# Scan of an RWKV recurrence: half of the heads change partition halves from level to level, and the inverse's factor is identity plus power

## What is computed

```python
def rwkv_step(S, inp):
    r, w, k, v, kk, a = inp
    sa = jnp.einsum('dbhvk,dbhk->dbhv', S, -kk)
    S = S * w[..., None, :] + sa[..., :, None] * (kk * a)[..., None, :] + v[..., :, None] * k[..., None, :]
    y = jnp.einsum('dbhvk,dbhk->dbhv', S, r)
    return S, y
```

## Time and profile before

| what | value |
|---|---|
| time, median of 3 runs | 4139.14 us (4133.52 to 4139.69) |
| time of the profiled execution | 4142.12 us |
| its span | 4140.3 us |
| granted clock, mean over the span | 0.936 |
| TensorE busy | 3631.0 us, 88% |
| VectorE busy | 2830.5 us, 68% |
| ScalarE busy | 1609.6 us, 39% |
| stage of the scan in the span | about 2785 to 3175 us |

### The profile page before, as it was taken

The page is one execution under the profiler, slowest core; times in us unless marked ns, Lnnn a source line. Parts: engine busy times, 40 slices in busy tenths (PEclk is TensorE's granted clock), DMA queues, the critical chain, the costliest instruction groups (busy, mean ns, idle before and its releaser), DMA issues. The chain is left out here.

```text
span 4140.3 us, 62371 instructions
## 1 busy us (share of the span) xinstructions
PE 3631.0 (88%) x24735; PEld 2927.8 (71%) x24735; DVE 2830.5 (68%) x3464; ACT 1609.6 (39%) x2136; POOL 72.4 (2%) x56
## 2 busy tenths in 40 slices
PE   6999996879959999948999776649999897999897
PEld 4888885767848888836888432319997676888786
DVE  4775325977559999978886588685555557667356
ACT  3222212545537777754333120253333133322244
POOL 0000000000020000010000000000000000000000
PEclk8999998999969999978999888779999998999999
DMA  5942225536579999953332331340111332222565
GB/s 199 337 166 92 88 76 194 192 112 214 181 278 420 413 411 411 399 194 102 102 122 102 124 123 69 117 166 26 42 34 63 102 117 77 82 91 73 187 192 170
DMA packets 262498, 689.49 MB, mean 167 GB/s; under 512 B 30136, under 2 KB 126072, under 8 KB 235754
## 3 DMA queue, kind: packets, MB, share of 16 engines
q1 hardware_dynamic: 226474, 559.75, 37.8%
q10 hardware_dynamic: 20528, 67.11, 4.3%
q0 software_dynamic: 15248, 59.14, 3.9%
HBM read 530.81 MB, written 172.96 MB: 170 GB/s over the span
## 5 line engine op out<-in xcount | busy, mean ns | idle before, releaser
L157 PE MATMUL g_ps<-h1T_hi,g_w_lo 128*128 128x512 f32 x448 | 175.4, 392 | 6.9 <-DVE g_w_lo L356 6.9
L1775 DVE TENSOR_TENSOR moe_wg_lo<-moe_wg,moe_wg_hi 128x2048 fp32r<-128x2048 f32 x68 | 153.1, 2288 | 35.6 <-ACT moe_wg_hi L1629 35.5
L159 PE MATMUL g_ps<-h1T_hi,g_w_hi 128*128 128x512 f32 x448 | 174.8, 390 | 0.0
L158 PE MATMUL g_ps<-h1T_lo,g_w_hi 128*128 128x512 f32 x448 | 174.8, 390 | 0.0
L4164 DVE TENSOR_TENSOR x3T_lo<-fd_w_raw,x3T_hi 128x1024 fp32r<-128x1024 f32 x66 | 80.8, 1224 | 122.6 <-ACT x3T_hi L4093 122.4
L1775 DVE TENSOR_TENSOR moe_wu_lo<-moe_wu,moe_wu_hi 128x2048 fp32r<-128x2048 f32 x68 | 152.9, 2288 | 16.3 <-ACT moe_wu_hi L1629 16.3
L1775 DVE TENSOR_TENSOR moe_wd_lo<-moe_wd,moe_wd_hi 128x2048 fp32r<-128x2048 f32 x66 | 148.3, 2289 | 14.9 <-ACT moe_wd_hi L1629 14.9
L2882 PE MATMUL rs_banks<-rs_pm,rs_qx 64*64 64x64 f32 x2048 | 157.2, 217 | 0.0
L157 PE MATMUL fd_acc<-x3T_hi,x3T_lo 128*128 128x512 f32 x352 | 139.2, 395 | 19.9 <-DVE x3T_lo L4167 19.9
L157 PE MATMUL g_ps<-x2T_hi,g_w_lo 128*128 128x512 f32 x352 | 139.8, 397 | 17.1 <-DVE g_w_lo L583 17.1
L157 PE MATMUL g_ps<-g_w_hi,h1T_lo 128*128 128x512 f32 x384 | 149.6, 390 | 0.0
(11 more groups left out here) (738 smaller groups left out, 10776.4 us busy)
## 6 DMA issues: line engine op xcount, KB each, us to landing
moe_wg<-in_exp_w_gate SPq DMA_DIRECT2D x68, 1024.0 KB
moe_wu<-in_exp_w_up SPq DMA_DIRECT2D x68, 1024.0 KB
moe_wd<-in_exp_w_down SPq DMA_DIRECT2D x66, 1024.0 KB
fd_w_raw<-in_ffn_w_down SPq DMA_DIRECT2D x66, 512.0 KB, 4.5
go_w_raw<-in_w_out SPq DMA_DIRECT2D x64, 512.0 KB, 4.4
g_w<-in_w_in SPq DMA_DIRECT2D x52, 512.0 KB, 4.8
g_w<-in_w_in SPq DMA_DIRECT2D x22, 1024.0 KB, 7.7
s_xs<-g_zero POOLq DMA_DIRECT2D x2, 8192.0 KB, 34.3
```

The costliest lines, as they stand in the source:

```text
L157: pe.matmul(out, l[1], r[0], start=(k == 0), stop=False)
L158: pe.matmul(out, l[0], r[1], start=False, stop=False)
L159: return pe.matmul(out, l[0], r[0], start=False, stop=(k == kt - 1))
L1775: v.tensor_tensor(lo[:, q * m:q * m + m], w[:, q * m:q * m + m], hi[:, q * m:q * m + m], ALU.subtract).then_inc(sem_lo, 1)
```

## The change

- Placement: a matrix of parity 0 stays in `home[b]`; one of parity 1 lies in `home[b]` at even levels and in the other half at odd ones (`place`). A product of parity 1 thus reads one half and writes the other, and the four kinds of matrices of a group use the four quadrants of the array.
- Groups are by direction (d = g) instead of parity.
- `qx` and `pm` become one tile `px` with three columns of 64: `pm`, `qm`, `xm`. PSUM has the three side by side too, one bank for each group and parity (`powers_of`).
- X is raised by `(I + power) X` in one product: `rx` = power + identity is made by VectorE at each level from 0 to 4, and the product of the next level has `rx` as weights. VectorE no longer adds the product to X; the new X comes with the copies.
- Each matrix has three matmuls of 64 columns at levels 1 to 3 instead of one of 128 and one of 64.
- Copies: for group 0 ScalarE copies parity 0 and VectorE parity 1, for group 1 ScalarE copies both; each copy has two or three times 64 columns for two slots (level 5: one times 64). VectorE's two adds for `rx` follow its copy and wait for ScalarE's copies.
- The first X is written in four operations instead of two, the parity-1 half of them into the other half of the partitions.

```diff
-        sc, pm, qx = s.sb("sc", [P, 2, ND, 2, P]), s.sb("pm", [P, ND, RC]), s.sb("qx", [P, ND, P])
+        sc, px = s.sb("sc", [P, 2, ND, 2, P]), s.sb("px", [P, ND, 3 * RC])
+        pm, qm, xm = (px[:, :, c * RC:c * RC + RC] for c in range(3))
+        rx, eye = s.sb("rx", [P, ND, RC]), s.sb("eye", [P, RC])
...
+        def powers_of(g, par):
+
+            return banks[:, 2 * g + par].rearrange("p n c -> p (n c)")[:, 0:6 * RC].rearrange("p (n c) -> p n c", c=3 * RC)
...
+        def columns(lv):
+
+            return slice(0, 2 * RC) if lv == 0 else slice(0, 3 * RC) if lv < NL - 1 else slice(2 * RC, 3 * RC)
+
+        def own(ap, g, par):
+
+            return ap[:, par * RP + 2 * g:par * RP + 2 * g + 2]
...
+        def place(b, par, lv):
+
+            return other[b] if par and lv % 2 else home[b]
...
                 if n:
-                    for g in range(2):
-                        pe.wait_ge(lv_dve, past(dve_level(n - 1, NL - 1, g)))
+                    pe.wait_ge(lv_act, past(act_at(n - 1, NL - 1, 3)))
+                    pe.wait_ge(lv_dve, past(dve_at(n - 1, NL - 1)))
...
                 for g in range(2):
                     if lv == 0:
                         pe.wait_ge(sc_ok, past(2 * n + 2))
+                        pe.wait_ge(p0_ok, past(n + 1))
                     else:
-                        if lv < NL - 1:
-                            pe.wait_ge(lv_q, past(q_level(n, lv - 1, g)))
-                        pe.wait_ge(lv_p1 if g else lv_p0, past(p_level(n, lv - 1)))
+                        pe.wait_ge(lv_act, past(act_at(n, lv - 1, 3 if g else 1)))
+                        if g == 0:
+                            pe.wait_ge(lv_dve, past(dve_at(n, lv - 1)))
+                    members = [(par * RP + g * 2 + a, a, b, par) for a in range(2) for par in range(2) for b in range(2)]
+
+                    def power(k, a, b, par):
+                        o = place(b, par, lv)
+                        return sc[o, n % 2, g * RP + 2 * a + b, par, 0:RC] if lv == 0 else qm[o, k]
+
+                    def to(a, b, par, c):
+                        return powers_of(g, par)[place(b, par, lv + 1), a, c * RC:c * RC + RC]
+                    if lv < NL - 1:
+                        for k, a, b, par in members:
+                            mm = pe.matmul(to(a, b, par, 0), power(k, a, b, par), pm[place(b, par, lv), k], start=True, stop=True)
+                    if lv < NL - 2:
+                        for k, a, b, par in members:
+                            mm = pe.matmul(to(a, b, par, 1), pm[place(b, par, lv), k], power(k, a, b, par), start=True, stop=True)
+                    if lv:
                         if lv == 1:
-                            pe.wait_ge(x1_ok, past(2 * n + 2))
-                        else:
-                            pe.wait_ge(lv_dve, past(dve_level(n, lv - 1, g)))
-                    for e in range(RP):
-                        for b in range(2):
-                            d, p, o, k = e // 2, e % 2 * 2 + b, home[b], g * RP + e
-                            q = sc[o, n % 2, d * RP + p, g, 0:RC] if lv == 0 else qx[o, k, 0:RC]
-                            if lv == 0:
-                                pe.matmul(p_q[g][o, e, 0:RC], pm[o, k], q, start=True, stop=True)
-                            elif lv < NL - 2:
-                                pe.matmul(p_q[g][o, e], pm[o, k], qx[o, k], start=True, stop=True)
-                            else:
-                                mm = pe.matmul(p_q[g][o, e, RC:P], pm[o, k], qx[o, k, RC:P], start=True, stop=True)
-                            if lv < NL - 1:
-                                mm = pe.matmul(p_p[g][o, e], q, pm[o, k], start=True, stop=True)
+                            pe.wait_ge(x1_ok, past(4 * n + 4))
+                        pe.wait_ge(lv_r, past(r_at(n, lv - 1, g)))
+                        for k, a, b, par in members:
+                            o = place(b, par, lv)
+                            mm = pe.matmul(to(a, b, par, 2), rx[o, k], xm[o, k], start=True, stop=True)
                     mm.then_inc(level, 1)
...
             def raise_power(n, lv):
-                for g in range(2):
-                    k = slice(g * RP, g * RP + RP)
+                c = columns(lv)
+                for g, par in ((0, 0), (1, 0), (1, 1)):
                     act.wait_ge(level, past(at_level(n, lv, g)))
-                    if lv < NL - 2:
-                        act.activation(qx[:, k, 0:RC], p_q[g][:, :, 0:RC], ACT.Copy).then_inc(lv_q, 1)
-                act.activation(pm[:, k], p_p[1][:, 0:RP], ACT.Copy).then_inc(lv_p1, 1)
+                    act.activation(own(px[:, :, c], g, par), powers_of(g, par)[:, :, c], ACT.Copy).then_inc(lv_act, 1)
...
+            for o in half:
+                v.tensor_copy(eye[o], ident[o, o])
+            v.drain()
...
                 for b in range(2):
-                    o = home[b]
-                    v.tensor_tensor(by_parity(qx[o])[:, :, :, RC:P], sides(sc[o, n % 2, :, :, 0:RC], b),
-                                    bc(ident[o, o].unsqueeze(1).unsqueeze(1), [64, 2, RP, RC]), ALU.add).then_inc(x1_ok, 1)
+                    for par in range(2):
+                        o = home[b]
+                        v.tensor_tensor(by_parity(xm[place(b, par, 1)])[:, par], sides(sc[o, n % 2, :, :, 0:RC], b)[:, par],
+                                        bc(eye[o].unsqueeze(1), [64, RP, RC]), ALU.add).then_inc(x1_ok, 1)
 
             def raise_power(n, lv):
+                c = columns(lv)
+                v.wait_ge(level, past(at_level(n, lv, 0)))
+                v.tensor_copy(own(px[:, :, c], 0, 1), powers_of(0, 1)[:, :, c]).then_inc(lv_dve, 1)
                 if lv < NL - 1:
-                    v.wait_ge(level, past(at_level(n, lv, 0)))
-                    v.tensor_copy(pm[:, 0:RP], p_p[0][:, 0:RP]).then_inc(lv_p0, 1)
-                for g in range(2 if lv else 0):
-                    k = slice(g * RP, g * RP + RP)
-                    v.wait_ge(level, past(at_level(n, lv, g)))
-                    if lv < NL - 2:
-                        v.wait_ge(lv_q, past(q_level(n, lv, g)))
-                    v.tensor_tensor(qx[:, k, RC:P], qx[:, k, RC:P], p_q[g][:, :, RC:P], ALU.add).then_inc(lv_dve, 1)
+                    v.drain()
+                    for g in range(2):
+                        v.wait_ge(lv_act, past(act_at(n, lv, 3 if g else 1)))
+                        both = [by_parity(t)[:, :, 2 * g:2 * g + 2] for t in (rx[:, :, :], pm)]
+                        v.tensor_tensor(both[0], both[1], bc(eye[:, :].unsqueeze(1).unsqueeze(1), [P, 2, 2, RC]), ALU.add
+                                        ).then_inc(lv_r, 1)
```

More of the change, by code:

```diff
@@ L2735, in rw_scan @@
         m_in, loaded = s.sem("m_in"), [s.sem(f"loaded{b}") for b in range(2)]
-        (turned, v_turned, p0_done, scored, level, z_done, u_done, s_done, y_done, bk_ok, v_ok, u_ok, lv_q,
-         lv_p0, lv_p1, p0_ok, sc_ok, x1_ok, lv_dve, zs_ok, s_ok, y_ok) = (s.sem(n) for n in (
+        (turned, v_turned, p0_done, scored, level, z_done, u_done, s_done, y_done, bk_ok, v_ok, u_ok, lv_act,
+         lv_dve, lv_r, p0_ok, sc_ok, x1_ok, zs_ok, s_ok, y_ok) = (s.sem(n) for n in (
              "turned", "v_turned", "p0_done", "scored", "level", "z_done", "u_done", "s_done", "y_done", "bk_ok",
-             "v_ok", "u_ok", "lv_q", "lv_p0", "lv_p1", "p0_ok", "sc_ok", "x1_ok", "lv_dve", "zs_ok", "s_ok", "y_ok"))
+             "v_ok", "u_ok", "lv_act", "lv_dve", "lv_r", "p0_ok", "sc_ok", "x1_ok", "zs_ok", "s_ok", "y_ok"))
         block = s.block()
@@ L2744, in wide @@
             return banks[:, n].rearrange("p n c -> p (n c)").rearrange("p (n c) -> p n c", c=P)
-        p_q, p_p = [wide(n) for n in range(2)], [banks[:, 2 + n] for n in range(2)]
+        def powers_of(g, par):
+            return banks[:, 2 * g + par].rearrange("p n c -> p (n c)")[:, 0:6 * RC].rearrange("p (n c) -> p n c", c=3 * RC)
         def chunk(d, j):
@@ L2818, in prepare @@
                 mm.then_inc(turned, 1)
-                if n:
-                    pe.wait_ge(lv_p0, past(p_level(n - 1, NL - 2)))
                 for d in range(2):
@@ L2825, in prepare @@
                 mm.then_inc(v_turned, 1)
-                if n:
-                    pe.wait_ge(lv_p1, past(p_level(n - 1, NL - 2)))
                 if n >= 2:
@@ L2907, in solve @@
                 pe.wait_ge(zs_ok, past(j + 1))
-                for g in range(2):
-                    pe.wait_ge(lv_dve, past(dve_level(j, NL - 1, g)))
+                pe.wait_ge(lv_act, past(act_at(j, NL - 1, 3)))
+                pe.wait_ge(lv_dve, past(dve_at(j, NL - 1)))
                 for d in range(2):
@@ L2912, in solve @@
                         k = slot(d, a, par)
-                        mm = pe.matmul(p_z[home[b], par, RP + d * 2 + a], qx[home[b], k, RC:P], zs[home[b], k],
+                        mm = pe.matmul(p_z[home[b], par, RP + d * 2 + a], xm[home[b], k], zs[home[b], k],
```

(4 more changed lines are left out.)

13 lines of the change are left out of this document (6 added, 7 removed).

## The result

The changed kernel takes 4155.85 us (median of 8 runs, 4144.98 to 4162.73), the kernel before 4139.41 us beside it (8 runs, 4133.52 to 4146.64): the ratio is 1.0033, 95% interval 1.0018 to 1.0048. So the change costs 16 us where I forecast a gain of 36. The profiled execution is the longest of the 8: 4162.73 us, span 4161.0. An execution that took over 1.5% longer than its kernel's fastest is left out of the medians and ratios of this document.

The account below looks back on a forecast made before the run. TensorE was taken as the bound (busy 88% of 4140.3 us). Per chunk 0.38 + 1.79 + 0.15 = 2.32 us, 34.8 us over 15 chunks, plus 1.3 us in chunk 0, gave 36 us less: 4103 us, range 4088 to 4124.

Parts of the forecast that it names:

- Pace of a quadrant, 14.6 ns: TensorE matmuls: a quadrant takes a pair each 58 ns whatever the others do, so four give 14.6 ns a pair.
- The level's loop of 2.07 us: Scan levels: from group 1's last matmul to its last in the next level, about 2.07 us against 2.68 before.
- Stalls of issue: Four-quadrant bursts: one stall of 0.3 to 0.5 us in 16 chunks; if one in each chunk, another 5 to 8 us go.
- 15 x 21.2 = 318: Scan: a period of 21.2 us between one chunk's p0 matmuls and the next.
- the 9.68 of the sum: Levels 1 to 5 of a chunk: level 1 at 1.40 plus 4 x 2.07 = 8.28, against 11.47 before.
- Pairs can't be issued that fast: Rival, levels: at 25 ns a pair a level's loop is 2.53 us; time 4130 to 4140; chance 5%.
- The clock rival: Rival, scan: idle of about 0.67 us a level lowers TensorE's clock to 1.2 GHz; mostly 4150 to 4250; chance 4%.
- DMAs are not touched: Whole kernel: the change leaves the DMAs as they were; no time was counted for them.
- The banks rival: Rival, levels: row halves take turns at a PSUM bank, 29.2 ns a pair; +6 us, 4145; chance 8%.
- The chain: Levels: evictions and VectorE's new add link levels, 2.09 us, or 2.03 by the powers; rival of a longer chain 6%.
- The wait of the update: State's update after level 0: TensorE stands some 0.5 us ahead of it, waiting for ScalarE's uv copies.
- Evictions of levels 4 and 5: Level 4 copies all 384 columns and level 5 waits for level 4's adds: both 2.07 us, before 1.87 and 1.56.

Follow-up runs that it names:

- the streams: Kernel before plus three streams of 512 matmul pairs ahead of p0 in chunks 5 and 11, outputs overwritten; 4226.42 us in a single execution.
- the third stream: Last of three 512-pair streams added to the kernel before, on two diagonal quadrants; whole run 4226.42 us.
- the second stream: Middle of three 512-pair streams added to the kernel before: four quadrants, banks fed from both row halves; 28.2 and 27.7 ns a pair, whole run 4226.42 us.
- the lean form: Changed kernel, parity 0 back to one 128-column matmul and VectorE's add, parity 1 unchanged; 4105.71 us with loads apart, 4109.16 us together.

## Why the prediction was wrong

*Pace of a quadrant, 14.6 ns: right* for any stretch of pairs inside one block (15 ns in the levels, 14.6 in the streams), *wrong as a rate to multiply with.* One slip on the way: (1.15 - 0.22 - 0.03) / 31 is 29.0 ns, not 29.2; the third stream gives 29.2.

*The step that failed* is the overlap of TensorE with its own program. The level's loop of 2.07 us counts 48 pairs at 14.6 ns, 0.70 us, as if the next instruction were always there. Stalls of issue stood outside the sum, bounded at one of 0.3 to 0.5 us a chunk. In their place the runs show a supply of 256 instructions each 3.3 to 3.5 us at best, and 2.7 us a chunk of idle time by issue. The 15 chunks take 371.0 us where 15 x 21.2 = 318 was forecast, 53 us more. By the four chunks at full clock about 37 us of that come with the breaks (15 x 2.5). The other 16 come with the low clock, which the sum put at nothing; that split is an estimate. The supply rate alone explains less: levels 1 to 5 hold 384 pairs, three blocks, which arrive in 3 x 3.47 = 10.4 us instead of the 9.68 of the sum, 11 us in 15 chunks.

*The rival "Pairs can't be issued that fast" was the right one in kind*, and I dismissed it on evidence that could not speak: the 32 pairs of L2832 and the 48 around ask are shorter than the 128 of one block. The sign stood in the earlier trace rows: a break in the middle of p0, with no operand missing. The rival's price, 4130 to 4140, was too low as well: its 25 ns is near the 27 measured, but a mean pace does not hold the waits that come behind a break. The Trainium skill's 25 ns from start to start (TensorE: Matmul & The Clock Gate, Back-to-back issue gap) lies near the 27 ns too; but inside a block 14.6 ns are seen, and the 27 are a mean with the breaks in it.

The supply alone is not the sum. The changed kernel has 87 packets in the 15 chunks, 5.8 a chunk, or 20.1 us at 3.47 each, less than the 24.7 that a chunk takes. My reading is that it has one block in stock: level 1 of the chunk shown starts at 2927.82, behind the slow update, and the stream breaks after 143 pairs, little more than one block. What the slow stretches (transposes, scores, update) leave over is then lost, and a break in one group delays its evictions and the next level, so that break and chain add up. In the kernel before the same queue brings 76 packets in 15 chunks, 5.1 to 23.6 us, where 17.6 us would do; there TensorE's matmuls are idle by issue for 0.4 us in all.

*The clock rival was right in part*, and I gave it too little. The clock falls 13 times in the 15 chunks, for 57 us in all at the 1.2 GHz level, 15% of them. Its own text said that one seventh of the scan at that level decides the sign. There is a slip in it: 10 us and the longer levels are 14 us a chunk over the forecast and so 12 over the kernel before, which makes it one sixth, and the whole scan at that level about 4317 instead of 4350. The estimate above is 16 us for the 57. I held that the gaps of my own chain were too short to bring the clock down. The run with the adds on VectorE contradicts that for a somewhat longer chain: 47.8 us low with hardly a break by issue, behind gaps of 0.3 to 1.2 us. In the changed kernel the falls stand behind breaks and chain gaps mixed.

*DMAs are not touched: wrong.* Their number is the same, but they compete with the instruction packets, which mattered little while TensorE used a block in 4.6 us.

*The banks rival is refuted* by the second stream. *The chain was right*, a little long: a chunk without the q product takes 20.18 us at least, and the chunk above 22.39 with 1.9 us of breaks in it. *The wait of the update* is 0.60 us from the last start, where I had 0.5. *Evictions of levels 4 and 5* depend on the rx add as I had it.

What stays open: what the clock costs beyond the estimate; which idle brings it down, as it falls behind 3 us in one piece and behind several of about one; and why the loads together cost nothing measurable in the lean form.

## What to carry to other kernels

Before a pace read from a short burst is multiplied, ask how many instructions in a row have ever run at it in the trace, and treat one unexplained "issue" in such a burst as the edge of a supply, to be priced for every block of the denser code. Where TensorE works in small pieces, count instructions as well as columns. Fewer instructions are not enough by themselves, though: with 11 matmuls a matrix and a longer chain of adds the time was 4146 us, with 12.5 and the evictions shared it was 4106. And ask which loads run beside dense TensorE code, even if no one seems to wait for them.

## What the hardware showed

- TensorE's instructions arrive 256 at a time, in one packet of 16 KB (12 packets more for 3072 instructions more). Packets started at least 3.3 to 3.5 us apart in every kernel here, however fast they were used up. The traces fit one block in stock. TensorE went on 2.2 to 3.0 us after the traced start of the packet that it lacked, and once 4.2 us, with the loads doubled.
- So 64x64 f32 pairs run at 14.6 ns for up to 128 pairs and at 27 to 28 ns for longer. At 29.2 ns (two quadrants) 512 pairs ran without a break in one place and at 32.4 ns with breaks in the other, behind two starved streams.
- Vector loads at over 90% of the DMA engines held the next packet back by about 2 us (5.6 us from packet to packet, 2903.28 to 2908.84, where 3.3 is the least), and the same loads doubled cost 14 us.
- Two row halves that write the same bank cost nothing: 128 pairs in 1.9 us with banks shared as with banks apart.
- The clock fell to the 1.2 GHz level in 13 places of the changed kernel's 15 chunks, and for 47.8 us in a kernel whose gaps were nearly all waits for copies and adds. It did not fall in the scan of the kernel before, nor in the two-quadrant run (18.8 us idle in 15 chunks, 1.3 us the longest).
